# Stick-breaking attention: running sums as two products of rounded parts in place of one four-byte product

## The chip, the core and the metric

The kernel runs on one core of a Trainium2 chip. The metric is the time of one execution on the device in microseconds (us).

## What is computed

The reference is a network of four layers over 512 tokens of width 1024: two layers of a first kind, then two hybrid layers. The change lies in the hybrid layers alone. One of their three mixers is a stick-breaking attention of four heads of size 64:

```python
z = einsum('bhqd,bhkd->bhqk', qb, k) * scale
past = kpos[None, :] < qpos[:, None]
log_keep = where(past, log_sigmoid(-z), 0.0)
log_later = cumsum(log_keep, axis=3, reverse=True) - log_keep
w = where(past, exp(log_sigmoid(z) + log_later), 0.0)
out = einsum('bhqk,bhkd->bhqd', w, v)
```

For each query this needs a sum over all later keys of the log terms. Everything is float32. The other mixers of these layers are a latent attention (MLA) and an RWKV recurrence; behind them come an output projection, a layer norm and a feed-forward part.

## The kernel before

The five engines run one program each, ordered by semaphores. Dense products with streamed weights (`chunk`) are made of rounded parts: a four-byte operand x is split by ScalarE into a high part, rounded to the type fp32r (`act(..., ACT.Copy)`), and by VectorE into a rest (x minus high part, also fp32r), and three fp32r matmuls high by high, high by rest, rest by high give the product. Other products, the stick-breaking ones among them, are plain float32 matmuls.

A stick-breaking head works on transposed scores (keys in partitions, queries in columns). The 512 keys are four blocks kt; block kt has 512 - 128 kt query columns, 1280 columns in all. The tiles are `zs` (scores, in LN), `tm` (a work tile, in LN) and `lk` (the log terms, in SM), each 128x1280. The steps of a head:

1. PE makes four score products; ScalarE and VectorE copy two blocks each to `zs`.
2. ScalarE: `tm` = ln(1 + exp(-|zs|)) in three instructions (Abs, Exp, Ln).
3. VectorE: `lk` = max(zs, 0) + tm in one instruction (L1212), then the diagonal blocks times a mask (four instructions, L1204). It then raises `st_l`.
4. PE waits for `st_l` and makes the running sums: block kt is the product of the triangle `REV` with its own block of `lk`, plus products of `ones` with the later blocks, accumulated in PSUM. These are ten products of 512, 384, 256 and 128 columns: kt 0 and 1 have seven (2048 columns), kt 2 and 3 have three (512 columns).
5. VectorE: `tm` = zs minus the sums, plus a mask on the diagonal. ScalarE: Exp. PE: ten products (20 records) with the values give the head's output.

The heads don't run alone. Each engine has a generator `stick()`, and one step of it (up to its next `yield`) is taken ahead of each quarter of a weight group of the three products `("r", c)`. On PE a quarter is 12 fp32r matmuls of 512 columns. In each of the engines' programs a head takes seven such turns: on PE scores in turn 1, nothing in turns 2 and 3, sums of kt 0 and 1 in turn 4, of kt 2 and 3 in turn 5, output in turn 7; on ScalarE copies in turn 1, step 2 in turn 2, the last Exp in turn 6; on VectorE step 3 in turn 3, step 5 in turns 4 and 5. There are 24 turns, so heads 0 to 2 and the first three turns of head 3 lie beside these products; then comes a fence of all engines, and the rest of head 3 runs among the strands of the other mixers, its sums right behind twelve transposes of the latent part. ScalarE and VectorE split the next weight group between turns 4 and 5, 8 and 9, 12 and 13, and so on, and evict finished chunks in the turns 5 to 8 of each chunk. `latent_norm` takes three turns beside head 0.

Of the kernel before, what the change touches and what calls it, by code (L numbers as in the profile page):

```python
# [245 lines left out]
def program(nc, ap):  # L246
# [3 lines left out]
    with ctx:  # L250
        def sb(name, w, dt=f32):
            return ctx.enter_context(nc.sbuf_tensor(name, [128, w], dt))
# [13 lines left out]
        CST = sb("CST", NC_CONST)  # L266
        PSM = sb("PSM", NPS + 28)
        P = sb("P", max(NPA, NPB))
        LN = sb("LN", 2560)
        SM = sb("SM", 1400)  # L270
        RAW = sb("RAW", 4096)
        HA, H2 = two("HA", 8192, "H2", 8192)
        SC, SPL = two("SC", 12288, "SPL", 12288)
# [32 lines left out]
        def bank(i, w=512):  # L306
            return psum[:, i * 512:i * 512 + w]
# [110 lines left out]
        F_ = R[:, 0:7168].rearrange("p (c s) -> p c s", c=14)  # L418
        off = [0, 512, 896, 1152]
        zs, tm, lk = LN[:, 0:1280], LN[:, 1280:2560], SM[:, 0:1280]  # L420
        CQ = HA[:, 0:1536].rearrange("p (c s) -> p c s", c=3)
        QM = HA[:, 1536:3072].rearrange("p (t h d) -> p t h d", t=4, h=4)
        KM = HA[:, 3072:4608].rearrange("p (t h d) -> p t h d", t=4, h=4)
# [87 lines left out]
        def tensor(pe):  # L511
# [6 lines left out]
            def mm(out, l_, r_, start=True, stop=True):  # L518
                return pe.matmul(out, l_, r_, start=start, stop=stop)  # L519
# [294 lines left out]
            def stick():  # L814
                for h in range(4):
                    rows = slice(64 * (h % 2), 64 * (h % 2) + 64)
                    for kt in range(4):
                        q0, W = kt * 128, 512 - kt * 128
                        if h:
                            pe.wait_ge(s.st_d, n["st_d"] - 3 + kt)  # L820
                        if h and kt == 3:
                            pe.wait_ge(s.st_y, n["st_y"])
                        mm(bank(kt, W), SQ[rows, 2 + h // 2, q0:q0 + 128], SQ[rows, h // 2, q0:512]).then_inc(s.st_s, 1)
                    yield
                    yield
                    yield
                    pe.wait_ge(s.st_l, n("st_l"))
                    pe.wait_ge(s.st_za, n("st_za", 2))
                    for kt in range(4):
                        W = 512 - kt * 128  # L830
                        for jt in range(kt, 4):
                            o = (jt - kt) * 128
                            ins = mm(bank(kt, W)[:, o:W], C("REV") if jt == kt else C("ones"),
                                     lk[:, off[jt]:off[jt] + 512 - jt * 128], jt == kt, jt == 3)
                        ins.then_inc(s.st_c, 1)
                        n("st_d")
                        if kt % 2:
                            yield
                    yield
                    pe.wait_ge(s.st_e, n("st_e"))  # L840
                    pe.wait_ge(s.st_d, n["st_d"])
                    for qt in range(4):
                        for kt in range(qt + 1):
                            a = off[kt] + (qt - kt) * 128
                            ins = mm(bank(3)[:, qt * 64:qt * 64 + 64], tm[:, a:a + 128],
                                     ZT[:, kt, 352 + h * 64:352 + h * 64 + 64], kt == 0, kt == qt)
                    ins.then_inc(s.st_o, 1)
                    n("st_y")
                    yield
                flags["sb"] = True  # L850
# [342 lines left out]
        def vector(v):  # L1193
# [430 lines left out]
            def stick():  # L1624
                for h in range(4):
                    for kt in range(4):
                        o, W = off[kt], 512 - kt * 128
                        k = n("st_s")
                        if kt % 2 == 0:
                            v.wait_ge(s.st_s, k)  # L1630
                            v.tensor_copy(zs[:, o:o + W], bank(kt, W)).then_inc(s.st_z, 1)
                    yield
                    yield
                    v.wait_ge(s.st_t, n("st_t"))
                    own(stt(lk, zs, 0.0, tm, ALU.max, ALU.add))
                    for kt in range(4):
                        d = lk[:, off[kt]:off[kt] + 128]
                        ins = tt(d, d, C("sbm"), ALU.mult)
                    ins.then_inc(s.st_l, 1)
                    yield  # L1640
                    for kt in range(4):
                        W = 512 - kt * 128
                        t_ = tm[:, off[kt]:off[kt] + W]
                        v.wait_ge(s.st_c, n("st_c"))
                        tt(t_, zs[:, off[kt]:off[kt] + W], bank(kt, W), ALU.subtract).then_inc(s.st_d, 1)
                        v.wait_ge(s.st_d, n("st_d"))
                        ins = tt(t_[:, 0:128], t_[:, 0:128], C("sbadd"), ALU.add)
                        if kt == 3:
                            ins.then_inc(s.st_x, 1)
                        if kt % 2:  # L1650
                            yield
                    yield
                    v.wait_ge(s.st_o, n("st_o"))
                    v.tensor_copy(YB[:, :, h * 64:(h + 1) * 64], v3(bank(3, 256), 4)).then_inc(s.st_y, 1)
                    yield
                flags["sb"] = True
# [273 lines left out]
        def scalar(a):  # L1930
# [255 lines left out]
            def stick():  # L2186
                for h in range(4):
                    for kt in range(4):
                        o, W = off[kt], 512 - kt * 128
                        k = n("st_s")  # L2190
                        if kt % 2:
                            a.wait_ge(s.st_s, k)
                            act(zs[:, o:o + W], bank(kt, W), ACT.Copy).then_inc(s.st_za, 1)
                            n("st_za")
                    yield
                    a.wait_ge(s.st_z, n("st_z", 2))
                    a.wait_ge(s.st_za, n["st_za"])
                    own(act(tm, zs, ACT.Abs))
                    own(act(tm, tm, ACT.Exp, scale=-1.0))
                    act(tm, tm, ACT.Ln, bias=C("eps", 3, 4)).then_inc(s.st_t, 1)  # L2200
                    yield
                    yield
                    yield
                    yield
                    a.wait_ge(s.st_x, n("st_x"))
                    act(tm, tm, ACT.Exp).then_inc(s.st_e, 1)
                    yield
                    n("st_o")
                    yield
                flags["sb"] = True  # L2210
# [128 lines left out]
            n("norms")  # L2339
            a.wait_ge(s.cst, 32)  # L2340
            turns(*[rms_tile(0, t) for t in range(4)])
            for l in range(2):
                transposed(lambda c: par(PS, PSM, f"n1_{l}", c, c + 1))
                high_parts()
                for c in (0, 1, 2, 4, 3):
                    chunk(2, by_turns((l, "z", c), sets[c % 2], lambda b: Z[:, b, c * 512:(c + 1) * 512]))
                    if c == 4:
                        og = Z[:, :, A_QK + 640:A_QK + 896]
                        a.wait_ge(s.ev, 10 * l + 8)
                        a.wait_ge(s.ea, n["ea"])  # L2350
                        act(og, og, ACT.Sigmoid)
                        logs()
                    if c == 1:
                        beside.append(qk_norm(l))
                    elif c == 2:
                        beside.append(qk_tail(l))
                while beside:
                    one_turn(beside)
                fence()
                mixer_a(l)  # L2360
                fence()
                transposed()
                fence()
                dense("rms")
                transposed(lambda c: par(PS, PSM, f"n2_{l}", c, c + 1))
                for p in range(4):
                    for q in range(2):
                        chunk(2)
                        for b in range(4):
                            i = p * 8 + q * 4 + b  # L2370
                            T = tl[i % 4]
                            a.wait_ge(s.mm, full_at[(l, "up", p, q), b])
                            act(T, bank(sets[q][b]), ACT.Relu).then_inc(s.fra, 1)
                            if i >= 10:
                                a.wait_ge(s.mm, full_at[(l, "down", (i - 10) // 8, 1), 3])
                            a.wait_ge(s.fv, n("fv"))
                            act(u2(i)[0], T, ACT.Copy).then_inc(s.uh, 1)
                    dense("rms" if p == 3 and l == 0 else None)
# [414 lines left out]
```

## Time and profile before

| what | value |
|---|---|
| median of three runs | 3230.69 us (3229.11 to 3238.85) |
| the profiled execution | 3235.39 us |
| its span, first to last instruction | 3233.6 us |
| mean granted TensorE clock | 0.916 |
| PE busy | 2880.6 us, 89% of the span |
| DVE (VectorE) busy | 1547.8 us, 48% |
| ACT (ScalarE) busy | 1044.6 us, 32% |

An instruction's duration reaches from its start to its end; matmuls overlap, so a run of them is costed by the time from its first start to the start of what follows. A float32 product stands in the trace as two matmul records, an fp32r product as one. PEclk is the granted clock: 1.00 is 2.4 GHz and 0.50 is 1.2 GHz, the two levels there are.

### The profile page before, as it was taken

To read this page: it belongs to the slowest core of one execution; us is meant where nothing else is said; L and a number is where in the kernel's file an instruction comes from. 1 tells how busy PE (TensorE), PEld (TensorE's weight loads), DVE (VectorE), ACT (ScalarE), POOL (GpSimd) and SP (SyncE) were. 2 spreads that over 40 slices of the span, in tenths; PEclk is the share of its full clock that TensorE was granted. 3 is DMA by queue.
4 is the path that set the end of the run, shared out by engine and by line. 5 is a ranking of instruction groups with operands and counts; after the bars stand their busy time and mean duration, and the time that the engine had idled before them with its cause. 6 is when DMAs were issued, how large, how long until landed. Compare 5 with 4: busy or idle time off the path is not lost.

```text
span 3233.6 us, 45203 instructions
## 1 busy us (share of the span) xinstructions
PE 2880.6 (89%) x19896; PEld 2379.5 (74%) x19896; DVE 1547.8 (48%) x2432; ACT 1044.6 (32%) x1554; POOL 191.7 (6%) x182
## 2 busy tenths in 40 slices
PE   7987999999888999998867789999888687789997
PEld 5876788878777888886557678888666387678885
DVE  3585533345565443424365554444533555554435
ACT  3333322232333322224232233223433432232323
POOL 0200000001100000000023200000000123000000
PEclk9977999999868999999878889999898798889998
DMA  4101222222003222221000123232210000223221
GB/s 163 53 1 62 80 103 94 102 78 84 9 1 108 99 98 98 89 86 40 1 1 29 51 89 108 92 104 78 84 52 1 1 3 29 92 78 104 91 98 46
DMA packets 30725, 216.59 MB, mean 67 GB/s; under 512 B 3648, under 2 KB 3776, under 8 KB 6080
## 3 DMA queue, kind: packets, MB, share of 16 engines
q1 hardware_dynamic: 30528, 213.69, 18.8%
q8 instruction: 157, 2.57, 0.3%
q14 instruction: 40, 0.33, 0.0%
HBM read 211.58 MB, written 2.10 MB: 66 GB/s over the span
## 4 chain that ended last, share of the span: by engine, by line
PE 80%; DVE 14%; ACT 4%; issue 2%; DMA 0%; DVEq 0%; SPq 0%; ACTq 0%
PE PS L519 76%; PE PS L522 3%; DVE SC L1204 2%; DVE SM L1215 1%; DVE X L1204 1%; DVE SM L1204 1%; DVE R L1204 1%; ACT LN L1943 1%; ACT SPL L1943 1%; DVE SPL L1204 1%; DVE HA L1204 1%; PE PS L1039 0%; PE PS L989 0%; ACT R L1943 0%; DVE SM L1209 0%
## 5 line engine op out<-in xcount | busy, mean ns | idle before, releaser
L519 PE MATMUL PS<-H,SPL 128*128 128x512 f32 (+1 forms) x4560 | 1056.4, 392 | 8.7 <-DVE SPL L1204 5.6
L519 PEld LDWEIGHTS PS<-H,SPL 128*128 128x128 f32 (+1 forms) x4560 | 853.5, 188 | 194.8 <-issue 8.2
L1204 DVE TENSOR_TENSOR SPL<-RAW,SPL 128x2048 fp32r<-128x2048 f32 (+2 forms) x194 | 434.3, 2240 | 768.3 <-ACT SPL L1943 768.3
L1943 ACT ACTIVATE SPL<-RAW 128x2048 fp32r<-128x2048 f32 (+2 forms) x194 | 362.0, 1869 | 922.4 <-PE PS L519 888.2
L519 PE MATMUL PS<-SPL,Uu 128*128 128x512 f32 x2592 | 589.8, 389 | 0.0
L519 PEld LDWEIGHTS PS<-SPL,Uu 128*128 128x128 f32 x2592 | 486.5, 188 | 101.0
L519 PE MATMUL PS<-SPL,H 128*128 128x512 f32 (+2 forms) x2112 | 463.6, 381 | 25.7 <-DVE SPL L1204 25.0
L519 PEld LDWEIGHTS PS<-SPL,H 128*128 128x128 f32 x2112 | 389.3, 193 | 99.4 <-issue 27.1
L1943 ACT ACTIVATE R<-PS 128x512 f32<-128x512 f32 (+2 forms) x182 | 104.6, 585 | 267.9 <-PE PS L519 243.1
L1204 DVE TENSOR_TENSOR X<-X,PS 128x512 f32<-128x512 f32 x112 | 76.7, 685 | 116.0 <-PE PS L519 116.0
L1943 ACT ACTIVATE Uu<-R 128x512 fp32r<-128x512 f32 x108 | 68.3, 632 | 141.2 <-DVE R L1204 141.2
L1204 DVE TENSOR_TENSOR Uu<-R,Uu 128x512 fp32r<-128x512 f32 x108 | 74.8, 693 | 79.8 <-ACT Uu L1943 79.8
L1204 DVE TENSOR_TENSOR R<-R,PS 128x512 f32<-128x512 f32 (+1 forms) x86 | 57.6, 670 | 105.5 <-PE PS L519 90.1
L519 PEld LDWEIGHTS PS<-R,SC 64*64 64x64 f32 (+1 forms) x1280 | 89.8, 182 | 19.7 <-issue 12.4
L522 PE MATMUL PS<-CST,R 128*128 128x128 f32 (+1 forms) x384 | 63.5, 332 | 41.3 <-DVE R L1208 23.4
L519 PE MATMUL PS<-R,SC 64*64 64x64 f32 (+1 forms) x1280 | 96.7, 269 | 2.4 <-ACT SC L1943 1.9
L519 PE MATMUL PS<-SM,CST 128*128 128x128 f32 (+5 forms) x224 | 61.9, 428 | 35.1 <-DVE SM L1204 35.1
L522 PEld LDWEIGHTS PS<-CST,R 128*128 128x128 f32 (+1 forms) x384 | 56.2, 173 | 49.2 <-issue 15.5
L1204 DVE TENSOR_TENSOR LN<-LN,PS 128x512 f32<-128x512 f32 (+3 forms) x74 | 42.5, 578 | 92.7 <-PE PS L519 92.6
L519 PE MATMUL PS<-R 64*64 64x64 f32 (+2 forms) x1760 | 71.7, 235 | 16.3 <-DVE R L1204 9.5
L519 PEld LDWEIGHTS PS<-SM,CST 128*128 128x128 f32 x224 | 44.1, 238 | 56.7 <-DVE SM L1204 37.9
L2449 POOL TENSOR_TENSOR HA<-HA,CST 128x64 f32<-128x64 f32 x16 | 4.6, 322 | 1313.4 <-ACT HA L1943 1313.4
(220 smaller groups left out, 2704.5 us busy)
## 6 DMA issues: line engine op xcount, KB each, us to landing
RAW<-in_wA SPq DMA_DIRECT2D x84, 1024.0 KB, 4.8
RAW<-in_wB SPq DMA_DIRECT2D x84, 1024.0 KB, 4.8
RAW<-in_wAo SPq DMA_DIRECT2D x8, 1024.0 KB, 4.8
RAW<-in_wBo SPq DMA_DIRECT2D x8, 1024.0 KB, 6.3
LN<-in_ln SPq DMA_DIRECT2D x4, 1024.0 KB, 6.1
P<-in_pB SPq DMA_DIRECT2D x2, 1920.0 KB, 8.9
RAW<-in_wBm SPq DMA_DIRECT2D x4, 704.0 KB, 4.1
X<-in_x SPq DMA_DIRECT2D x4, 512.0 KB, 5.0
```

What stands on the lines that cost most here:

```text
L519: return pe.matmul(out, l_, r_, start=start, stop=stop)
L522: return pe.transpose(out, i, C("ident"))
L1204: return v.tensor_tensor(out, a, b, o)
L1215: return v.tensor_reduce(out=out, in_=a, op=o, axis=AX.X)
L1943: return a.activation(out, in_, f, scale=scale)
L2449: return g.tensor_tensor(out, a, b, o)
```

## The change

It splits `lk` as the dense operands are split. ScalarE writes its rounded high part `lk_hi` over `tm`, VectorE writes the rest `lk_lo` over `lk` itself, and the triangle and the ones are copied once, at the start, to an fp32r tile `TRI`. Each of the ten float32 products of a head becomes two fp32r products.

```diff
-        LN = sb("LN", 2560)
-        SM = sb("SM", 1400)
+        LN, LNr = two("LN", 2560, "LNr", 2560)
+        SM, SMr = two("SM", 1400, "SMr", 1400)
+        TRI = sb("TRI", 256, f32r)
...
+        lk_hi, lk_lo = LNr[:, 1280:2560], SMr[:, 0:1280]
...
-                    pe.wait_ge(s.st_l, n("st_l"))
+                    pe.wait_ge(s.st_l, n("st_l", 2))
...
-                            ins = mm(bank(kt, W)[:, o:W], C("REV") if jt == kt else C("ones"),
-                                     lk[:, off[jt]:off[jt] + 512 - jt * 128], jt == kt, jt == 3)
+                            tri = TRI[:, 0:128] if jt == kt else TRI[:, 128:256]
+                            cols = slice(off[jt], off[jt] + 512 - jt * 128)
+                            mm(bank(kt, W)[:, o:W], tri, lk_hi[:, cols], jt == kt, False)
+                            ins = mm(bank(kt, W)[:, o:W], tri, lk_lo[:, cols], False, jt == 3)
...
                     ins.then_inc(s.st_l, 1)
+                    n("st_l", 2)
+                    v.wait_ge(s.st_t, n("st_t"))
+                    tt(lk_lo, lk, lk_hi.bitcast(f32), ALU.subtract).then_inc(s.st_l, 1)
                     yield
...
                     act(tm, tm, ACT.Ln, bias=C("eps", 3, 4)).then_inc(s.st_t, 1)
                     yield
+                    a.wait_ge(s.st_l, n("st_l", 2) - 1)
+                    act(lk_hi, lk, ACT.Copy).then_inc(s.st_t, 1)
                     yield
...
+            act(TRI[:, 0:128], C("REV"), ACT.Copy)
+            act(TRI[:, 128:256], C("ones"), ACT.Copy)
```

`two` gives two names of different type to the same memory.

## Rows read from the trace of the kernel before

**Rows 1.** The page: busy time by engine, and the chain that ended last.

```profile
PE 2880.6 (89%) x19896; PEld 2379.5 (74%) x19896; DVE 1547.8 (48%) x2432; ACT 1044.6 (32%) x1554; POOL 191.7 (6%) x182
...
PE 80%; DVE 14%; ACT 4%; issue 2%; DMA 0%; DVEq 0%; SPq 0%; ACTq 0%
```

**Rows 2.** PE's timeline, first hybrid layer: start, us, operation, [idle before <-releaser].

```profile
1457.74 8.45 PE L519 MATMUL PS<-H,SPL 128*128 128x512 f32 x36
1468.21 5.41 PE L519 MATMUL PS<-SM,CST 128*128 128x512 f32 x14 [2.02 <-DVE SM L1204]
1473.37 3.00 PE L519 MATMUL PS<-H,SPL 128*128 128x512 f32 x12
1476.21 1.04 PE L519 MATMUL PS<-SM,CST 128*128 128x256 f32 x6
1477.00 5.73 PE L519 MATMUL PS<-H,SPL 128*128 128x512 f32 x24
1483.25 2.44 PE L519 MATMUL PS<-R,LN 128*128 128x64 f32 x20 [0.52 <-ACT LN L1943]
...
1539.97 6.00 PE L519 MATMUL PS<-SM,CST 128*128 128x512 f32 x14 [6.24 <-DVE SM L1204]
```

**Rows 3.** PE's waits, 1455 to 1600 us: waiter <- releaser: total, times, longest.

```profile
PE PS L519 <- DVE SM L1204: 11.7, 3, 6.2
PE PS L522 <- DVEq L1219: 3.6, 1, 3.6
```

**Rows 4.** The same for the second hybrid layer, 2365 to 2530 us.

```profile
PE PS L519 <- DVE SM L1204: 16.8, 3, 7.5
PE PS L522 <- DVEq L1219: 4.9, 1, 4.9
```

**Rows 5.** Timeline of ACT and DVE ahead of head 1's sums.

```profile
1498.83 1.36 ACT L1942 ACTIVATE LN<-LN,CST 128x1280 f32<-128x1280 f32 x1
1500.23 1.49 DVE L1212 SCALAR_TENSOR_TENSOR SM<-LN 128x1280 f32<-128x1280 f32 x1 [1.57 <-ACT LN L1942]
1501.76 0.90 DVE L1204 TENSOR_TENSOR SM<-SM,CST 128x128 f32<-128x128 f32 x4
```

**Rows 6.** Groups, ACT and DVE, 1455 to 1600 us: busy, mean ns | idle before.

```profile
L1943 ACT ACTIVATE LN<-LN 128x1280 f32<-128x1280 f32 x12 | 15.2, 1269 | 18.1 <-DVE LN L1204 16.7 <-DVE LN L1631 1.3
...
L1204 DVE TENSOR_TENSOR SPL<-RAW,SPL 128x2048 fp32r<-128x2048 f32 x5 | 11.5, 2293 | 11.4 <-ACT SPL L1943 11.4
...
L1212 DVE SCALAR_TENSOR_TENSOR SM<-LN 128x1280 f32<-128x1280 f32 x4 | 6.0, 1488 | 1.6 <-ACT LN L1942 1.6
```

**Rows 7.** PE in the eight stretches of the seven first sums: from:to us, busy, PEclk.

```profile
1468.21:1473.37 5.16, 5.16 (x14) 0.67 0.00 0
...
2460.68:2466.88 6.20, 6.20 (x15) 0.55 0.00 0
2499.40:2503.33 3.93, 3.93 (x16) 0.88 0.00 0
sum 41.96, PE 41.95; mean PE 5.24
```

**Rows 8.** PE in the eight stretches of the three last sums, the sum alone.

```profile
sum 6.49, PE 6.49; mean PE 0.81
```

**Rows 9.** PE in three stretches of one kind of matmul each, at full clock.

```profile
1457.74:1466.19 8.45, 8.45 (x37) 1.00 0.36 124
1433.58:1435.02 1.44, 1.44 (x14) 1.00 0.00 0
1483.25:1485.50 2.25, 2.25 (x20) 1.00 0.71 295
```

**Rows 10.** DVE's timeline ahead of the fence in head 3.

```profile
1573.56 0.75 DVE L1212 SCALAR_TENSOR_TENSOR R<-PS,PSM,SC 128x512 f32<-128x512 f32 x1
```

**Rows 11.** ACT's timeline: the start of the kernel, and the second layer ahead of an Exp.

```profile
20.09 2.42 ACT L1943 ACTIVATE H<-PS,PSM 128x512 fp32r<-128x512 f32 x4 [5.40 <-PE PS L522]
...
2431.38 1.28 ACT L1943 ACT_TABLE_LOAD   x1
```

## The prediction

> **What bounds the kernel now.** I read the page first. PE is busy 89% of the span and holds 80% of the chain that ended last [rows 1], so cheaper PE work counts only where PE is not waiting for others, and dearer work of other engines counts only where PE waits for it. The next view is PE's timeline around the stick-breaking heads [rows 2]. The reader should see that head 0 of the first hybrid layer has 36 covering matmuls (8.45 us) behind its scores, then a wait of 2.02 us released by DVE's SM, the tile `lk`, and then the seven first sums (kt 0 and 1). In head 2 the wait is 6.24 us. The list of waits gives the rest: three waits for `lk` in the first layer, 11.7 us, and three in the second, 16.8 us; head 3 has none there, but a wait of 3.6 and 4.9 us for DVE's fence [rows 3, 4]. Ahead of the fence DVE makes head 3's `lk` and then one eviction, 0.75 us [rows 10]; behind it PE starts again. So in all eight heads (four, two layers) PE stands still until DVE has `lk`, and the chain in front of that is serial: Ln ends at 1500.19, DVE's maximum starts at 1500.23 and its masks at 1501.76, PE starts at 1502.71 [rows 5], 0.04 to 0.05 us at each hand-over. The covering matmuls are used up: whatever is added to this chain is added to the kernel.
>
> **What the change adds.** Per head, between the masks and the sums, lie now an ACT copy of 128x1280 and a DVE subtraction of 128x1280, one after the other, each after a semaphore.
> - The copy: ACT needs 1269 ns for an instruction of this shape without a tile operand beside it [rows 6]: 1.27 us. It lies in ACT's turn 3, behind the head's Ln. Nothing of the stream stands between in heads 0 and 1; in head 2 the split and eviction are done before DVE's masks, since DVE's own low part waits for that split.
> - The subtraction: 1488 ns for DVE's two-operand instruction of this width, and 2293 ns at 2048 columns with an fp32r output [rows 6], which at the same slope is 1.49 too: 1.49 us.
> - Two hand-overs of 0.04: 0.08 us.
>
> Sum 2.84 us a head. In head 3 the wait moves ahead of DVE's eviction and thus of the fence, so PE's restart is later by the same amount: ACT's last `mu_part` is held behind the copy but done (0.6 us) while DVE subtracts. Eight heads: 8 x 2.84 = 22.7 us, all on the path. Queued behind ACT's new wait are otherwise only splits that wait for PE, and behind DVE's new wait `latent_norm`'s products (0.95 us in head 0) and the subtractions that wait for the sums anyway. No DMA is issued or moved; SP's stream is far ahead of its use by PE. ACT's two copies to `TRI` fall in a gap of 5.40 us in which ACT waits for PE [rows 11]; without that cover they would cost once at most what two instructions of four times their width take there, 2 x 2.42 / 4 = 1.2 us.
>
> **What it removes.** The seven first sums take 41.96 us in eight heads [rows 7]. Their stretch times its granted clock is the same everywhere: 5.16 x 0.67, 6.20 x 0.55 and 3.93 x 0.88 give 3.46, 3.41 and 3.46. So the work is 3.44 us at 2.4 GHz (1.68 ns a column), and the other 41.96 - 8 x 3.44 = 14.4 us are the price of the 1.2 GHz that is granted after the wait. The three last sums take 6.49 us, 0.81 a head, at full clock [rows 8].
>
> For the fp32r products three prices at full clock follow from [rows 9]: 8.45 / 36 = 0.235 us at 512 columns, 1.44 / 12 = 0.120 at 256; 0.177 at 384 lies between. No fp32r matmul of 128 columns is in the trace, and eight of a head's twenty have that width. The bounds: the line through 512 and 256 gives 0.062; a 128-column float32 product costs 128 x 1.68 = 0.215. Between them stands a row of this very kind of bound: the float32 records with 64 columns and a 128x128 stationary tile follow each other at 2.25 / 20 = 0.112 us although they have half the columns, so there the loading of the stationary tile sets the pace. I take 0.112 for 128 columns, since each fp32r product loads its own 128x128 tile too, and that row is the nearest in size.
>
> First sums: two of 512, four of 384, four of 256 and four of 128: 0.47 + 0.71 + 0.48 + 4 x 0.112 = 2.11 us (1.91 at 0.062; 2.52 at 0.215). Last sums: two of 256, four of 128: 0.24 + 0.45 = 0.69 (0.49; 1.10).
> - Saved in the first sums: 3.44 - 2.11 = 1.33, times 8 = 10.6 us.
> - Saved in the last sums: 0.12 in six heads, 0.7 us. In head 0 of each layer it buys nothing: the output there waits 0.52 us for ACT's Exp [rows 2], whose chain (split, low part, subtraction, Exp) starts at matmuls ahead of the last sums.
> - The 14.4 us of low clock I leave as they are. Low clock has a length of its own: the stretches after the short waits lost 1.7 us to it (5.16 - 3.44), the one after the longest 2.8, the one behind the transposes of head 3 0.5. Shorter sums leave the rest of the low stretch to the dense matmuls behind. Longer waits push the loss up, but also let more of the low stretch pass in the wait. Bounds: 3 us less, if all go as the shorter waits (1.4), to 6 us more, if all heads go as those after the longer ones (2.5 each, 20 in all).
>
> Balance: 22.7 - 10.6 - 0.7 = +11.4 us. The profiled execution took 3235.39 us, 1.8 more than its span; 3246.8 is 1.0035 of it. The median is 4.7 us lower, and 1.0035 of the median is **3242 us**.
>
> **What the skill says.** The Trainium skill (TensorE: Matmul & The Clock Gate, Back-to-back issue gap) gives about 81 ns for each load-and-matmul pair of 128 columns in a stream; it measured another type, and no row here shows it. By it the first sums would save 1.46 a head and the last 0.25, 13.1 us, and the balance would be +9.6 us. The same notes (FP8 and Floating Point Precision, TensorE Precision Notes) say a true float32 product is four passes through the array, where a rounded one is one; by that the change halves ten products' columns, saves 1.72 in eight heads and 0.40 in six, and ends at +6.5 us. [Rows 9] show more than bare columns, 0.120 us for 256, so I hold the rows' price.
>
> **The rivals.**
> - *Narrow products cheap* (0.062 us): saves 12.2 + 1.9 = 14.1 us, balance +8.6, 3239 us. For it: the line from 512 to 256 columns is nearly through zero, so the load is hidden down to there. Against: the 0.112 row. Chance 0.25.
> - *Narrow fp32r products as dear as float32 ones* (0.215 us, each of them, now twice as many): saves 8 x 0.92 = 7.4, loses 0.29 in six heads, 1.7; balance +17.0, 3248 us. For it: nothing here shows an fp32r product under 256 columns at any better price. Against: the price hardly rises above the columns from 512 to 256. Chance 0.28.
> - *The low clock passes in the wait* (the other side): the waits grow from 2.0..7.5 to 4.9..10.4 us, and the low clock that is granted for PE's standing still might be over before the sums begin. If all 14.4 us of loss went, the balance would be 11.4 - 14.4 = -3.0 us, 3228 us. It decides from a loss reduced by 11.4 us. Against: after the longest wait the loss was the largest, 2.8 [rows 7]. Chance 0.05.
> - *The copy makes ACT reload its tables*: a load is 1.28 us [rows 11]; in eight heads ahead of the copy +10, balance +22, 3252 us. Against: the load in that row stands ahead of an Exp, and Copy, which makes every split, is used between all the other functions. Chance 0.05.
> - The forecast as worked out: 0.35; 0.02 for what I don't see.
>
> **How the numbers follow.** 0.3% is 9.7 us, about what a measurement of this kernel can tell from none. The forecast (+11.4, give or take 3) is above it 7 times in 10, the cheap rival (+8.6) nearly 4 in 10, the dear one and the reloads always. Slower: 0.25 + 0.09 + 0.28 + 0.05, about 0.66; same: 0.29; faster: 0.05, the clock rival. The range takes both bounds of the narrow price, each with some clock: +8.6 less 3 is 3236, +17.0 plus 4 is 3252.
>
> **What would show it.** In the profile after: PE waits for DVE's SM of about 20 us in the first layer and 25 in the second, and waits for the fence of about 6.5 and 7.7; eight ACT instructions LN<-SM 128x1280 of 1.27 us, eight DVE ones SM<-SM,LN of 1.49, the second starting 0.04 after the first; 160 matmul records with TRI where 160 with SM,CST were; the first sums in some 2.1 us times full clock, 3.9 with the low one; last sums 0.69. The prediction is wrong if the waits grow by less than 2.8 a head (some of the chain was covered), if the narrow products start further apart or closer than 0.11 us, or if the low clock's loss in the sums and the matmuls behind them moves by more than 5 us.

## The result, and the profile after

| comparison | before | the change | ratio, 95% interval |
|---|---|---|---|
| first, ten runs of it | 3233.28 us | 3247.41 us (3229.89 to 3257.77) | 1.0055 (1.0029 to 1.0082) |
| again, twelve runs | 3234.83 us | 3248.34 us (3236.89 to 3257.10) | 1.0041 (1.0022 to 1.0060) |

The change makes the kernel slower, by some 0.4 to 0.6%, 13 to 18 us; the medians, of which the ratio is not the exact quotient, lie 14.1 and 13.5 us apart. One of the ten executions of the kernel before took 4411 us, and the ratio is of the others. The forecast was 3242 us in a range of 3236 to 3252. The profiled execution took 3246.42 us, with a span of 3244.6 against 3233.6, 11.0 us more.

The page after, its busy times and its chain:

```profile
PE 2868.8 (88%) x19896; PEld 2380.4 (73%) x19896; DVE 1559.7 (48%) x2440; ACT 1054.8 (33%) x1564; POOL 191.6 (6%) x182
...
PE 79%; DVE 14%; ACT 5%; issue 1%; DMA 0%; DVEq 0%; SPq 0%; ACTq 0%
```

PE is busy for 11.8 us less than in [rows 1] and the span is 11.0 us longer: the loss is waiting. DVE and ACT have 11.9 and 10.2 us more, above all eight subtractions and eight copies. PE's list of waits says where, first hybrid layer (1455 to 1620 us), then the second (2370 to 2560 us), to be read against [rows 3, 4]:

```profile
PE PS L521 <- DVE SMr L1208: 20.2, 3, 9.1
PE PS L524 <- DVEq L1223: 6.4, 1, 6.4
...
PE PS L521 <- DVE SMr L1208: 25.3, 3, 10.3
PE PS L524 <- DVEq L1223: 7.7, 1, 7.7
```

Four waits a layer, 37.0 us before and 59.6 now. The next views show what they wait for: the groups of ACT and DVE in the first layer, and then their timeline ahead of head 0's sums.

```profile
L1950 ACT ACTIVATE LNr<-SM 128x1280 fp32r<-128x1280 f32 x4 | 5.1, 1269 | 13.6 <-DVE SM L1208 13.6
...
L1208 DVE TENSOR_TENSOR SMr<-SM,LNr 128x1280 fp32r<-128x1280 f32 x4 | 6.0, 1492 | 5.3 <-ACT LNr L1950 5.3
```

```profile
1468.05 0.90 DVE L1208 TENSOR_TENSOR SM<-SM,CST 128x128 f32<-128x128 f32 x4
...
1468.98 1.27 ACT L1950 ACTIVATE LNr<-SM 128x1280 fp32r<-128x1280 f32 x1 [3.31 <-DVE SM L1208]
...
1470.28 1.49 DVE L1208 TENSOR_TENSOR SMr<-SM,LNr 128x1280 fp32r<-128x1280 f32 x1 [1.34 <-ACT LNr L1950]
```

The copy starts 0.03 us behind the masks, DVE stands idle for it for 1.34 us, the subtraction starts 0.03 behind the copy and PE 0.06 behind the subtraction. The first row below is the restart of PE in head 0, on its timeline:

```profile
1471.83 0.79 PE L521 MATMUL PS<-LNr,TRI 128*128 128x512 f32 x1 [4.85 <-DVE SMr L1208]
...
1479.09 0.28 PE L521 MATMUL PS<-LNr,TRI 128*128 128x256 f32 x1
1479.21 0.28 PE L521 MATMUL PS<-SMr,TRI 128*128 128x256 f32 x1
1479.33 0.22 PE L521 MATMUL PS<-LNr,TRI 128*128 128x128 f32 x1
1479.39 0.27 PE L521 MATMUL PS<-SMr,TRI 128*128 128x128 f32 x1
1479.50 0.27 PE L521 MATMUL PS<-LNr,TRI 128*128 128x128 f32 x1
1479.61 0.28 PE L521 MATMUL PS<-SMr,TRI 128*128 128x128 f32 x1
1479.72 5.67 PE L521 MATMUL PS<-H,SPL 128*128 128x512 f32 x24
```

From start to start, the three last sums take 0.63 us (0.79 in head 0 before), with 0.12 us for a product of 256 columns, and for one of 128 columns 0.06 once and 0.11 three times. The seven first sums, in the same windows as [rows 7]:

```profile
1471.83:1475.72 3.89, 3.89 (x14) 0.50 0.00 0
...
1585.74:1588.07 2.33, 2.33 (x17) 0.90 0.00 0
...
2473.41:2477.20 3.79, 3.79 (x14) 0.52 0.00 0
2512.22:2515.43 3.21, 3.21 (x16) 0.63 0.00 0
sum 28.78, PE 28.78; mean PE 3.60
```

28.78 us in place of 41.96. Time times clock is 1.95, 2.10, 1.97 and 2.02 in these rows, 1.98 in the mean over the eight, against 3.44: the work fell by 1.46 us a head. Behind three of the four waits of a layer the clock is at its low level through the whole of the sums, where before the sums outlasted it. In two heads of the six the twelve matmuls behind the sums now also run at the low level for a while. These windows are those twelve after heads 0 and 1 of the first layer, the kernel before in the first fence, the changed one in the second:

```profile
1473.37:1476.21 2.84, 2.84 (x15) 1.00 0.00 0
1507.87:1510.71 2.84, 2.84 (x15) 1.00 0.00 0
```

```profile
1475.72:1479.09 3.37, 3.37 (x13) 0.81 0.00 0
1512.32:1516.17 3.85, 3.85 (x14) 0.71 0.00 0
```

In head 2 and in the three heads of the second layer they take 2.8 to 2.9 us, so nothing is lost there. The last views are of the whole turns of the four heads, from head 0's scores to the first products of values and weights behind head 3, in both layers. Before, and after:

```profile
1455.39:1597.45 142.06, 122.79 (x516) 0.93 0.07 23
2365.67:2522.71 157.04, 128.52 (x516) 0.89 0.06 21
```

```profile
1456.17:1604.45 148.28, 117.47 (x516) 0.88 0.06 22
2376.55:2535.32 158.77, 118.73 (x516) 0.87 0.06 20
```

The turns take 299.1 us before and 307.1 with the change, 8.0 more; the other 3.0 of the 11.0 us lie where the two programs differ by nothing but the two short copies to `TRI`. Of the 8.0, 6.2 fall on the first layer and only 1.7 on the second. There the execution of the kernel before lost more to the low clock: behind head 1 the same wait of 1.93 us for the Exp stands in both traces, but only before did the clock go low behind it, and the head's output and the twelve matmuls behind took 8.36 us in place of the 5.20 with the change:

```profile
2434.00:2436.96 2.96, 2.96 (x20) 0.75 0.03 6
2436.96:2442.36 5.40, 5.40 (x15) 0.50 0.00 0
```

### The profile page after: what moved, and what is told of

Same layout as the page of the kernel before. It is cut to its first block, busy times and chain, and to the rows that moved or that the text cites. A ratio compares the mean times of both kernels' runs of the same rounds, so it can differ in the third digit from the quotient of the medians.

```text
span 3244.6 us, 45221 instructions
## 1 busy us (share of the span) xinstructions
PE 2868.8 (88%) x19896; PEld 2380.4 (73%) x19896; DVE 1559.7 (48%) x2440; ACT 1054.8 (33%) x1564; POOL 191.6 (6%) x182
## 3 DMA queue, kind: packets, MB, share of 16 engines
q1 hardware_dynamic: 30528, 213.69, 18.8%
## 4 chain that ended last, share of the span: by engine, by line
PE 79%; DVE 14%; ACT 5%; issue 1%; DMA 0%; DVEq 0%; SPq 0%; ACTq 0%
PE PS L521 76%; PE PS L524 3%; DVE SC L1208 2%; DVE SM L1219 1%; DVE X L1208 1%; DVE SM L1208 1%; DVE R L1208 1%; ACT LN L1950 1%; ACT SPL L1950 1%; DVE SPL L1208 1%; DVE HA L1208 1%; PE PS L1043 0%; PE PS L993 0%; ACT R L1950 0%; DVE SM L1213 0%
## 5 line engine op out<-in xcount | busy, mean ns | idle before, releaser
L521 PEld LDWEIGHTS PS<-R 64*64 64x64 f32 (+1 forms) x1760 | 60.5, 144 | 29.3 <-issue 9.6
L521 PE MATMUL PS<-HA 64*128 64x128 f32 (+3 forms) x256 | 62.1, 465 | 20.0 <-DVE R L1208 13.7
```

## The experiments

The theory: each head pays a chain of 2.84 us that nothing covers, and gets back what the cheaper products save. The rivals: the low clock decides (it passes in the longer waits, or takes more in them), the narrow products decide, or the waits are not what bounds these turns.

### The chain alone

ACT's copy and DVE's subtraction stay, the result of the subtraction goes to a place that nobody reads, and the sums are the ten float32 products of before, behind both.

```diff
-                            tri = TRI[:, 0:128] if jt == kt else TRI[:, 128:256]
-                            cols = slice(off[jt], off[jt] + 512 - jt * 128)
-                            mm(bank(kt, W)[:, o:W], tri, lk_hi[:, cols], jt == kt, False)
-                            ins = mm(bank(kt, W)[:, o:W], tri, lk_lo[:, cols], False, jt == 3)
+                            ins = mm(bank(kt, W)[:, o:W], C("REV") if jt == kt else C("ones"),
+                                     lk[:, off[jt]:off[jt] + 512 - jt * 128], jt == kt, jt == 3)
...
-                    tt(lk_lo, lk, lk_hi.bitcast(f32), ALU.subtract).then_inc(s.st_l, 1)
+                    tt(lk_hi, lk, lk_hi.bitcast(f32), ALU.subtract).then_inc(s.st_l, 1)
```

> The chain without the new products: ACT's copy and DVE's subtraction stand ahead of the sums, which wait for both, but the ten products stay float32 products of lk. Path theory (every head pays the whole chain, and the change's products gave back some 11 us): the waits are those of the changed kernel (20.2 and 25.3 us for DVE in the two layers, 6.4 and 7.7 at the fence) and the time is 22.7 us over before, ratio 1.0070. Rival, the low clock passes in the longer waits: the waits grow the same, but the seven first sums take less than their 41.96 us and the ratio stays under 1.0045. Rival, the products gave nothing: the ratio is that of the changed kernel, 1.0055 or less, with the sums at the same cost as there.

Ratio 1.0081 (1.0062 to 1.0099), 26 us: slower than the change itself. Its waits, first layer and second, are those of the changed kernel to the tenth:

```profile
PE PS L521 <- DVE LNr L1206: 20.2, 3, 9.1
PE PS L524 <- DVEq L1221: 6.4, 1, 6.4
...
PE PS L521 <- DVE LNr L1206: 25.3, 3, 10.3
PE PS L524 <- DVEq L1221: 7.7, 1, 7.7
```

The waits are all due to the chain, and both rivals of this run fall: the seven first sums take 43.70 us in eight heads, not less than their 41.96 of before, and the ratio is above the change's.

### The products alone

DVE writes the log terms rounded in the instructions it has; no copy, no subtraction. The second product of each pair takes a stationary tile of zeros, so the sums are those of rounded terms.

The edit, against the kernel before:

```diff
-                            ins = mm(bank(kt, W)[:, o:W], C("REV") if jt == kt else C("ones"),
-                                     lk[:, off[jt]:off[jt] + 512 - jt * 128], jt == kt, jt == 3)
+                            tri = TRI[:, 0:128] if jt == kt else TRI[:, 128:256]
+                            cols = slice(off[jt], off[jt] + 512 - jt * 128)
+                            mm(bank(kt, W)[:, o:W], tri, lk_lo[:, cols], jt == kt, False)
+                            ins = mm(bank(kt, W)[:, o:W], TRI[:, 256:384], lk_lo[:, cols], False, jt == 3)
...
-                    own(stt(lk, zs, 0.0, tm, ALU.max, ALU.add))
+                    own(stt(lk_lo, zs, 0.0, tm, ALU.max, ALU.add))
...
+            act(TRI[:, 256:384], C("ones"), ACT.Copy, scale=0.0)
```

> The products without the chain: DVE writes lk rounded (fp32r) in the instructions that it has anyway, there is no copy and no subtraction, and each running sum is the product of the rounded lk with triangle or ones plus a second product with a stationary tile of zeros in place of the rest's. So the sums are of rounded terms. Path theory: waits as before (11.7 and 16.8, 3.6 and 4.9 us), 11 us saved in the sums, ratio 0.9965. If narrow products were as dear as float32 ones, 6 us saved, 0.998. If the low clock takes back what the products save, under 4 us, 0.999 to 1.000.

Ratio 0.9937 (0.9914 to 0.9960), -20 us, more than the 11 expected; the interval reaches to -13. The waits are those of before (11.7 and 3.6 us, 16.8 and 4.9). The two halves of the change together, +26 and -20, make +6 us, and each has some 7 us of uncertainty; that holds the change's second ratio (+13) but doesn't settle the last few us. In the profiled executions the turns of the heads took 25.1 us more than before with the chain alone and 15.2 less with the products alone, +9.9 together, and 8.0 more with the change.

### One rounded product

The same without the second product, so ten products a head and no rest. The edit, against the run before it:

```diff
-                            mm(bank(kt, W)[:, o:W], tri, lk_lo[:, cols], jt == kt, False)
-                            ins = mm(bank(kt, W)[:, o:W], TRI[:, 256:384], lk_lo[:, cols], False, jt == 3)
+                            ins = mm(bank(kt, W)[:, o:W], tri, lk_lo[:, cols], jt == kt, jt == 3)
```

> As the run with the products alone, but without the second product: ten rounded products a head, no rest, so sums of rounded terms. Path theory: first sums about 1.0 us at full clock in place of 3.44, last sums 0.35 in place of 0.81, some 22 us saved, ratio 0.993. If the matmuls behind the sums then run at the low clock for as long as the sums would have, the saving is still that, since work at 1.2 GHz costs double wherever it lies; if the clock stays low for longer after less work, 15 us, 0.995.

Ratio 0.9915 (0.9894 to 0.9936), -27 us against 22 expected. Halving the products again is worth about 7 us beyond the run with pairs, where the two expectations had put 11; the two intervals overlap, so by the times alone that step is not shown. In the traces the turns are 7.1 us shorter: PE has 10.9 us less to do, and the low clock took 3.2 us more. What PE's sums can still give is small beside the chain.

### High parts first

PE multiplies with the high parts as soon as ACT has made them, and waits for the rest only then.

```diff
-                    pe.wait_ge(s.st_l, n("st_l", 2))
...
+                    def part(kt, src, hi):
...
+                            ins = mm(bank(kt, W)[:, o:W], tri, src[:, off[jt]:off[jt] + 512 - jt * 128],
+                                     hi and jt == kt, not hi and jt == 3)
+                        return ins
...
+                    pe.wait_ge(s.st_t, n("st_t", 2))
+                    pe.wait_ge(s.st_za, n("st_za", 2))
+                    for pair in ((0, 1), (2, 3)):
+                        for kt in pair:
+                            part(kt, lk_hi, True)
+                        if pair[0] == 0:
+                            pe.wait_ge(s.st_l, n("st_l", 2))
+                        for kt in pair:
+                            part(kt, lk_lo, False).then_inc(s.st_c, 1)
+                            n("st_d")
+                        yield
```

> The changed kernel with another order on PE: kt 0 and 1 first take all their products with the high parts, as soon as ACT has copied, and only then wait for DVE's rest. The subtraction (1.49 us) then lies beside some 2 us of matmuls at 1.2 GHz. Path theory: PE starts 1.53 us earlier in heads 0 to 2 of each layer, 9 us less than the changed kernel; head 3 gains nothing, because the fence waits for the subtraction. Ratio 1.002 to 1.003 against before. If the chain were not what PE waits for, the ratio stays at 1.0055.

Ratio 1.0004 (0.9981 to 1.0027), level with before. Waits in the first layer and the second:

```profile
PE PS L521 <- ACT LNr L1956: 15.6, 3, 7.5
PE PS L524 <- DVEq L1229: 6.4, 1, 6.4
...
PE PS L521 <- ACT LNr L1956: 20.7, 3, 8.8
PE PS L524 <- DVEq L1229: 7.7, 1, 7.7
```

4.6 us less in each layer, 1.53 a head in three heads, and the fence unmoved, as expected. The ratio fell by 0.0037 to 0.0051, 12 to 16 us, where the waits account for 9; in the profiled executions the turns became 8.7 us shorter.

### Later turns, rounded and float32

The steps of a head move: log terms (and copy and subtraction) to turn 4, all the sums to turn 5. PE has 48 covering matmuls in place of 36, and head 3's log terms are made behind the fence. The edit on PE, the other engines' alike:

```diff
                     yield
                     yield
                     yield
+                    yield
                     pe.wait_ge(s.st_l, n("st_l", 2))
...
-                        if kt % 2:
-                            yield
+                    yield
                     yield
```

> The changed kernel with the steps of a head in later turns: ACT's copy and DVE's log terms with their subtraction in turn 4, all ten pairs of sums in turn 5, output still in turn 7. PE then has 48 covering matmuls behind the scores in place of 36 (2.8 us more), and head 3's log terms are made behind the fence, beside the latent strand. Path theory: the waits of heads 0 to 2 shrink by 2.8 us each (20.2 to 11.7 and 25.3 to 16.8), the fence waits of 6.4 and 7.7 to about 1.5 each, 28 us less than the changed kernel in all, some 12 us less than before: ratio 0.996. Rival: the later sums make the output wait for Exp and give it back: ratio 1.002 or more.

> The kernel before (float32 sums, no split) with the same later turns. Path theory: without the 2.84 us of the split the waits of heads 0 to 2 come to nearly 0, 0.6 and 3.4 us in the first layer and 1.7, 1.9 and 4.7 in the second, and head 3's fence waits go to 1.5: 24 us less than before, ratio 0.9925, and the low clock with its 14 us in the sums largely goes too, 0.990. The rounded version with the same turns is then slower than this one: the change would lose wherever the chain is not covered. Rival (products matter more than the chain): this run is slower than the moved rounded one.

The changed kernel in the later turns: 0.9965 (0.9943 to 0.9987). The kernel before in the later turns: 0.9944 (0.9921 to 0.9967). The waits in the first layer, the rounded version in the first fence, the float32 one in the second:

```profile
PE PS L521 <- DVE SMr L1208: 9.9, 2, 6.4
PE PS L521 <- issue: 3.8, 2, 3.0
...
PE PS L524 <- DVEq L1223: 1.6, 1, 1.6
```

```profile
PE PS L519 <- DVE SM L1204: 4.3, 2, 3.5
...
PE PS L522 <- DVEq L1219: 1.6, 1, 1.6
```

Head 0's wait is listed here under "issue" (3.0 of 3.8 us; in the float32 version 0.2). In the rounded version heads 1 and 2 of each layer wait 2.7 us less and head 0 only 1.8. With the fence that makes 24.4 us less waiting than in the changed kernel, where 28 had been expected, and 25 to 29 us less time. In the float32 version the heads wait less by the same 2.7 and 1.8 us, the waits fell by 18.8 us in all and the time by 18, where 24 to 32 had been expected. The two intervals overlap, and the turns in the profiled executions differ by 2.2 us (281.5 rounded, 279.3 float32): that float32 is the faster of the two in these turns is likely, but not shown.

### Filler in the wait

Matmuls that nobody reads run in PE's wait for the log terms.

```diff
+                    if h < 3:
+                        pe.wait_ge(s.st_z, n("st_z", 2))
+                        for _ in range(32):
+                            mm(bank(2)[:, 256:512], TRI[:, 0:128], TRI[:, 0:256])
+                    else:
+                        n("st_z", 2)
                     pe.wait_ge(s.st_l, n("st_l", 2))
```

> The changed kernel with 32 matmuls of 256 columns (3.8 us at full clock) into unused columns of bank 2 ahead of the wait for the log terms in heads 0 to 2, nothing reads them. They lie inside waits of 4.85 to 10.35 us, so the sums start when they started, but PE has been at work for most of the wait. If the clock is granted by how busy PE was, the first sums of heads 0 and 1 go from 3.9 us at 0.50 to 2.0 us at 1.00, and 6 to 10 us are won over the changed kernel, ratio 1.003. If the clock doesn't depend on it, the time is that of the changed kernel.

Ratio 1.0026 (1.0004 to 1.0048), 5 to 9 us less than the change; the interval overlaps both of the change's, so a gain is not shown. The sums of heads 0 to 2 in the first layer:

```profile
1454.05:1456.19 2.14, 2.14 (x15) 1.00 0.00 0
1488.34:1491.91 3.57, 3.57 (x14) 0.56 0.02 5
1526.61:1530.51 3.90, 3.90 (x15) 0.50 0.00 0
```

In head 0, where 1.02 us of the wait are left behind the filler, the sums run at 2.4 GHz and take 2.14 us in place of 3.89. In head 1 2.47 us are left and the gain is small; in head 2 5.24 us are left and it is nothing. The length that is left doesn't decide alone: in the second layer the sums took 3.90, 2.68 and 3.91 us behind 3.57, 3.74 and 6.52 us, the best of them behind the middle one. So a wait costs its length and then, often, the low clock behind it, and work without any use in the wait can take the second part away in a single head. Over the whole turns it did not pay: the first layer's became 2.4 us shorter than the changed kernel's, the second's 4.5 us longer, because 15.2 us were lost to the low clock there in place of 10.5.

### Later turns and high parts first

With `part` as in the run with high parts first:

```diff
...
+                    pe.wait_ge(s.st_t, n("st_t", 2))
+                    pe.wait_ge(s.st_za, n("st_za", 2))
+                    for kt in range(4):
+                        part(kt, lk_hi, True)
+                    pe.wait_ge(s.st_l, n("st_l", 2))
+                    for kt in range(4):
+                        part(kt, lk_lo, False).then_inc(s.st_c, 1)
+                        n("st_d")
```

> The moved rounded version with all products of the high parts ahead of the wait for the rest. In the run that had this order in the old turns PE's waits fell by 1.53 us in heads 0 to 2. Path theory: the same again, 6 heads, 9 us off the moved rounded version (0.9965), and in head 3, where nothing is made ahead of the fence now, up to 1.5 us more a layer: ratio 0.993 to 0.994, level with the moved float32 version (0.9944). Rival: in the later turn the split is already covered, and the ratio stays at 0.9965.

Ratio 0.9913 (0.9890 to 0.9936), 28 us under before and the lowest ratio of the versions that keep the rest. Against the float32 sums in the same turns (0.9944, to 0.9921 at the lowest) the intervals overlap, so that the split itself gains anything there is not shown; the turns in the profiled executions are 6.8 us shorter (272.5 against 279.3). PE's timeline, head 1:

```profile
1483.12 11.17 PE L521 MATMUL PS<-H,SPL 128*128 128x512 f32 x48
1496.34 2.74 PE L521 MATMUL PS<-LNr,TRI 128*128 128x512 f32 x10 [2.04 <-ACT LNr L1955]
1498.88 2.00 PE L521 MATMUL PS<-SMr,TRI 128*128 128x512 f32 x10
```

The wait is 2.04 us (6.29 in the changed kernel; before it stood on the line below), the rest's products follow the high parts' without a gap, and both sets of ten take 4.4 us from start to start.

```profile
1502.71 5.41 PE L519 MATMUL PS<-SM,CST 128*128 128x512 f32 x14 [3.47 <-DVE SM L1204]
```

### Narrower products

The products with the last key block take 64 of their 128 columns, so half of that block's terms are left out of the sums.

```diff
-                            cols = slice(off[jt], off[jt] + 512 - jt * 128)
-                            mm(bank(kt, W)[:, o:W], tri, lk_hi[:, cols], jt == kt, False)
-                            ins = mm(bank(kt, W)[:, o:W], tri, lk_lo[:, cols], False, jt == 3)
+                            cols = slice(off[jt], off[jt] + (512 - jt * 128 if jt < 3 else 64))
+                            W_ = W if jt < 3 else o + 64
+                            mm(bank(kt, W)[:, o:W_], tri, lk_hi[:, cols], jt == kt, False)
+                            ins = mm(bank(kt, W)[:, o:W_], tri, lk_lo[:, cols], False, jt == 3)
```

> One look at what sets the pace of the 128-column fp32r products: in the changed kernel the products with the last key block (jt = 3), 128 columns wide, take only their first 64 columns, so half of that block's terms are left out of the running sums. If the columns set the pace, eight products a head start 0.027 us closer at full clock and the seven first sums fall from 1.98 to 1.87 us times clock, the last from 0.63 to 0.52. If the loading of the 128x128 stationary tile sets it (0.11 us for each load that a narrow product must hide), both stay where they are. Time within the scatter of the changed kernel either way.

Head 0's first and last sums:

```profile
1477.75:1481.61 3.86, 3.86 (x15) 0.50 0.00 0
1484.94:1485.54 0.60, 0.60 (x8) 1.00 0.00 0
```

3.86 and 0.60 us with half the columns, against 3.89 and 0.63. The single execution took 3255.32 us, within the scatter of the changed kernel. The columns are not what narrow products cost: three of four stay 0.11 us apart.

### The change again

> The changed kernel once more, for a narrower interval against before. Its first ratio was 1.0055 (1.0029 to 1.0082); the sum from the waits (+23) and the sums at full clock (-12.8) says +10 us, 1.003, and the two one-sided runs together (+26, -20 us) say +6, 1.002. If these hold, the ratio of this run is between 1.002 and 1.004; if something is left out of the sum, it stays at 1.0055.

Ratio 1.0041 (1.0022 to 1.0060), 13 us, at the upper edge of what was expected; the interval holds both values that were to be told apart, 1.003 and 1.0055.

The traces tell more than the ratios. This table has one profiled execution of each version and the turns of the four heads in both layers together, in us. "Low clock" is half of the time in which PE was busy while the clock was granted at 0.50; "work" is what is left of the turns without idle time and low clock.

| version | turns | PE idle | low clock | work |
|---|---|---|---|---|
| before | 299.1 | 47.8 | 21.0 | 230.3 |
| the change | 307.1 | 70.9 | 19.6 | 216.6 |
| the change again | 307.3 | 70.8 | 19.8 | 216.6 |
| the chain alone | 324.2 | 70.4 | 23.6 | 230.2 |
| the products alone | 283.9 | 48.2 | 18.9 | 216.8 |
| one rounded product | 276.8 | 48.8 | 22.1 | 205.9 |
| high parts first | 298.3 | 61.6 | 20.0 | 216.7 |
| filler in the wait | 309.2 | 47.9 | 21.7 | 239.6 |
| later turns, rounded | 281.5 | 47.1 | 17.7 | 216.7 |
| later turns, float32 | 279.3 | 30.5 | 19.1 | 229.8 |
| later turns, high parts first | 272.5 | 37.9 | 17.7 | 217.0 |

The two executions of the changed kernel agree to 0.2 us in the turns, yet their spans are 3244.6 and 3235.3 us. All of that difference lies outside the turns, where both run the same program, and 8.3 us of it is low clock.

## Why the prediction was right

**The chain: 2.84 us a head, 22.7 in all, nothing covers it.** Right in every part (the line on which PE starts at 1502.71, which [rows 5] leaves out, stands above): copy 1.27, subtraction 1.49, four waits a layer longer by 22.6 us in all. The run with the chain alone has the same waits and none of the gain. The fence of head 3 moved as forecast (3.6 to 6.4, 4.9 to 7.7).

**The first sums: 3.44 to 2.11 us at full clock.** Right in size. By time times clock 1.98 was measured, so the saving is 1.46 a head in place of 1.33, 11.7 us in place of 10.6. But that product is lowest where the clock is low: 1.95 at 0.50, 2.10 at 0.90, and in the filler's head 0, at 1.00 from end to end, 2.14.

**The narrow products: 0.112 us.** Right in size, and the cause is borne out in part. At 128 and at 64 columns alike, narrow products behind a narrow one are 0.11 us apart, so the columns don't set the pace. The loads of the stationary tile in the changed kernel's last sums start at 1479.21, 1479.33, 1479.44, 1479.55 and 1479.66, 0.11 apart as well; that they set the pace is inferred from this. The start that follows a narrow product behind one of 256 columns comes after 0.06, but then the product behind the narrow ones pays, here one of 384 columns with 0.22 in place of the 0.177 of the prediction:

```profile
1455.21 0.22 PE L521 MATMUL PS<-LNr,TRI 128*128 128x128 f32 x1
1455.27 0.27 PE L521 MATMUL PS<-SMr,TRI 128*128 128x128 f32 x1
1455.38 0.39 PE L521 MATMUL PS<-LNr,TRI 128*128 128x384 f32 x1
1455.60 0.34 PE L521 MATMUL PS<-SMr,TRI 128*128 128x384 f32 x1
```

Both rivals on this price fall: at full clock the first sums would have taken 1.91 or 2.52 us, and the last 0.49 or 1.10. The Trainium skill (TensorE: Matmul & The Clock Gate, Back-to-back issue gap) has 81 ns for a pair of 128 columns, in a section that names no type. It lies between the two spacings of 0.06 and 0.11, and with it the sum gives 1.98 and 0.56 us, where 1.95 to 2.14 and 0.63 were measured. The Trainium skill (FP8 and Floating Point Precision, TensorE Precision Notes) has four passes for a true float32 product; what the prediction made of it, 1.72 us for the first sums, is below every measured value. That a rounded product is one pass isn't spelled out in that section; the rows bear it out nearly, 0.46 ns a column at 512 columns against 1.68.

**The last sums: 0.69 us.** 0.63 was measured; in head 0 it bought nothing: the output's wait for Exp grew from 0.52 to 0.74 us, as said.

**The low clock: left as it was.** In the profiled executions this holds, within 1.5 us: over the whole turns 21.0 us were lost to it before and 19.6 and 19.8 with the change. In the sums and the matmuls behind them it looks like no change at all (28.78 - 8 x 1.98 = 12.9 us in the sums and 0.5 and 1.0 behind two heads, 14.4 as before), but that leaves out the 3.2 us which the kernel before lost behind head 1 of the second layer. One step of the working was loose: the bound of 3 us less goes by a loss of 1.4 us a head behind the short waits, where the prediction's own rows give 1.7, which is 0.8 us less in all.

**The balance: +11.4 us.** In the turns it was +8.0 and +8.2: 23 us of waiting, 13.7 us less work and 1.5 or 1.2 us less low clock. The prediction had 22.7, 11.3 and 0. So the profiled pair's 11.0 us lie beside 11.4 by luck, since 3.0 of them come from outside the turns; the second execution of the changed kernel was just 1.7 us above before. Over all executions the difference is larger, 13 to 18 us by the ratios. The mean granted clock is 0.919 in 63 executions of the kernel before and 0.912 in 22 of the changed one, a wider gap than the profiled pair's 0.916 and 0.913. So it is likely that low clock makes up the 5 to 10 us that the turns don't show, for which the prediction had allowed up to 6. No trace shows where it lies, nor that the longer waits bring it about: this stays open. With the chain alone the turns lost 2.6 us more to the low clock than before, which covers most of its surplus (26 for 22.7).

**Rivals.** The clock that passes in the wait is refuted: behind the waits of 4.85 to 10.35 us the sums ran at the low level nearly from end to end, PEclk 0.50 to 0.52. No load of ACT's tables lies between Ln and the copy in the timeline of head 0, and there are 36 such loads in the whole trace, before and after alike.

## What to carry to other kernels

Before making an operation cheaper by preparing its operands, look at what its engine waits for ahead of it: here the preparation lay on that wait, 2.84 us, and the cheaper products gave 1.5 to 1.6 us back. If the preparation comes in parts, start with the part that is ready, so that the second hides behind the first's work, and move the step to where there is cover: with both, the same split became 0.9% faster than the kernel before. Most of that is the move, which made the unsplit kernel 0.6% faster by itself; that the split adds to it is not shown. A product with few columns didn't get cheaper with fewer of them, 0.11 us at 128 and at 64, so counting columns flatters it. And where one kernel's executions scatter by more than the change, compare the stretches that the change touches: they agreed to 0.2 us in two traces whose spans differ by 9.3.

## What the runs showed of the hardware

- The spread between executions of one kernel goes with the granted clock. Of the kernel before, 3208.69 us went with a mean clock of 0.926 and 3248.31 us with 0.911; of the changed kernel 3236.89 with 0.918 and 3257.10 with 0.907. One profile against another can thus mislead by 10 us: the two of the changed kernel lie 9.3 us apart, and outside the turns of the heads they lost 163.7 and 155.4 us to the low clock.
- Between the start of an fp32r product of 128 columns and the next start lie 0.11 us, with 64 columns as well, where it stands behind another narrow one, and 0.06 us (0.03 with 64 columns) where it stands behind one of 256; then a product of 384 columns behind the narrow ones takes 0.22, the one after it 0.18.
- Behind a wait of 1.02 us the sums were at 2.4 GHz, behind those of 4.85 us and more in heads 0 to 2 of the changed kernel at 1.2 GHz nearly from the first to the last (PEclk 0.50 to 0.52). In between the length doesn't decide alone: behind 3.74 us, with filler ahead, the first products were at 2.4 GHz, behind 2.47 at 1.2 GHz; and behind the same wait of 1.93 us the clock soon fell to 1.2 GHz before and stayed at 2.4 GHz with the change.
